# Decoder block: low parts written over the raw weight slabs, six slabs of two buffers, gelu loads one slab ahead

## What is computed

```python
def mixer_sublayer(h, ...):            # h: 16 meta tokens and 512 tokens, D_MODEL = 1024
    z = h @ w_in + b_in                # q, k, v of two attentions, forget gate, two gates
    oa = sliding_window_attention(...)
    ob = forgetting_attention(...)
    merged = sigmoid(ga) * (oa @ w_pa) + sigmoid(gb) * (ob @ w_pb)
    return merged @ w_o

def peer_ffn(h, w_q, sub_keys, u, v):  # 8 heads, 128 x 128 experts, 16 chosen per head
    q = h @ w_q                        # scores of 2 x 128 sub-keys per head
    ...                                # top 16 of each half, top 16 of their sums -> expert, g
    a = gelu(h . u[expert]) * g
    return sum(a * v[expert])
```

## Time and profile before

| | |
|---|---|
| median of 3 runs | 1650.83 us (1649.65 to 1651.99) |
| span of the profiled execution | 1647.4 us |
| PE busy | 1607.1 us, 98% |
| DVE busy | 1333.8 us, 81% |
| ACT busy | 739.8 us, 45% |
| DMA, mean over the span | 266 GB/s |

### The profile page before, as it was taken

How to read it: one execution, slowest core, us unless ns; L and a number is a source line. 1 busy time by engine, 2 the same in 40 slices (tenths; PEclk the granted TensorE clock), 3 DMA queues, 4 the chain that set the end, 5 groups by cost and what they waited for, 6 DMA issues and landing times. The chain is left out here.

```text
span 1647.4 us, 26956 instructions
## 1 busy us (share of the span) xinstructions
PE 1607.1 (98%) x9840; PEld 1487.9 (90%) x9840; DVE 1333.8 (81%) x2850; ACT 739.8 (45%) x1298; POOL 455.8 (28%) x319
## 2 busy tenths in 40 slices
PE   6999999999899999999999999999999999999996
PEld 4897766788788999999999999999999999999996
DVE  4534656565688989999999989769999989898998
ACT  5314644442433535767667744343333333333331
POOL 0000000000011051431233233424554554556740
PEclk9999999999999999999999999999999999999998
DMA  4561111123154596998999899999999999999992
GB/s 150 122 200 39 52 52 52 49 85 98 65 160 135 162 381 209 330 352 255 326 334 341 286 368 340 371 409 378 406 405 405 405 405 403 391 404 400 405 405 102
DMA packets 192500, 438.01 MB, mean 266 GB/s; under 512 B 18744, under 2 KB 102912, under 8 KB 191984
## 3 DMA queue, kind: packets, MB, share of 16 engines
q1 hardware_dynamic: 80928, 226.94, 38.3%
q0 software_dynamic: 44080, 161.06, 26.4%
q10 hardware_dynamic: 67360, 48.28, 8.9%
HBM read 380.08 MB, written 56.13 MB: 265 GB/s over the span
## 5 line engine op out<-in xcount | busy, mean ns | idle before, releaser
L495 PE MATMUL psS<-hT_lo,hi 128*128 128x368 f32 (+2 forms) x1448 | 496.9, 343 | 0.7 <-DVE hT_lo L1111 0.7
L496 PE MATMUL psS<-hT_hi,lo 128*128 128x368 f32 (+2 forms) x1448 | 488.1, 337 | 0.0
L497 PE MATMUL psS<-hT_hi,hi 128*128 128x368 f32 (+2 forms) x1448 | 486.1, 336 | 0.0
L486 DVE TENSOR_TENSOR lo<-raw,hi 128x1024 fp32r<-128x1024 f32 x322 | 393.5, 1222 | 113.2 <-ACT hi L482 105.9
L482 ACT ACTIVATE hi<-raw 128x1024 fp32r<-128x1024 f32 x322 | 339.0, 1053 | 136.5 <-PE psS L497 96.1
L612 POOL DMA_INDIRECT gat<-in_u_rows,idx x144 | 214.7, 1491 | 393.2 <-DVE gat L1290 213.3
L495 PEld LDWEIGHTS psS<-hT_lo,hi 128*128 128x128 f32 x1448 | 272.0, 188 | 23.6 <-issue 11.7
L612 POOL DMA_INDIRECT gat<-in_v_exp,idx x144 | 223.4, 1551 | 228.5 <-DVE gat L1290 146.3
L497 PEld LDWEIGHTS psS<-hT_hi,hi 128*128 128x128 f32 x1448 | 272.2, 188 | 11.6
L496 PEld LDWEIGHTS psS<-hT_hi,lo 128*128 128x128 f32 x1448 | 272.1, 188 | 9.1
L844 ACT ACTIVATE act_hi<-act_t 128x368 fp32r<-128x368 f32 x128 | 65.6, 512 | 289.7 <-DVE act_t L1342 283.1
(11 more groups left out here) (337 smaller groups left out, 2562.1 us busy)
## 6 DMA issues: line engine op xcount, KB each, us to landing
raw<-in_u_exp SPq DMA_DIRECT2D x128, 512.0 KB
raw<-in_v_exp SPq DMA_DIRECT2D x128, 512.0 KB
gelu_dram<-gelu ACTq DMA_DIRECT2D x128, 184.0 KB
gates_dram<-gates ACTq DMA_DIRECT2D x92, 256.0 KB
gel_in<-gelu_dram SPq DMA_DIRECT2D x128, 184.0 KB
raw<-in_w_merge SPq DMA_DIRECT2D x24, 512.0 KB
raw<-in_w_proj SPq DMA_DIRECT2D x18, 512.0 KB
gate_even<-gates_dram SPq DMA_DIRECT2D x24, 384.0 KB
```

What stands on the lines that cost most here:

```text
L486: nc.vector.tensor_tensor(lo[:, n % RING, :], raw[:, n % RING, :], hi[:, n % RING, :].bitcast(F32), ALU.subtract).then_inc(lo_done, 1)
L495: nc.tensor.matmul(out_ap, w_h, x_l, start=start, stop=False)
L496: nc.tensor.matmul(out_ap, w_l, x_h, start=False, stop=False)
L497: return nc.tensor.matmul(out_ap, w_h, x_h, start=False, stop=stop)
```

## The change

`raw` and `lo` are placed at the same address, so that `lo` is written over `raw`, element by element. The memory that three rings of four took now holds two rings of SLABS = 6. A load can no longer go into its buffer when lo(n-4) is done: load n waits until PE has finished slab n-6. hi(n) waits for the landing and for the end of slab n-6 in place of n-4; its place in ACT's program and that of lo(n) in DVE's are as they were. In the v stage the `gel_in` load behind the load of slab v is now that of v+1.

```diff
@@ placing of the buffers
-        raw, hi, lo = place(ctx, raw=([P, RING, D], F32), hi=([P, RING, D], F32R), lo=([P, RING, D], F32R))
+        hi, = place(ctx, hi=([P, SLABS, D], F32R))
+        with ExitStack() as s:
+            raw, = place(s, raw=([P, SLABS, D], F32))
+        lo, = place(ctx, lo=([P, SLABS, D], F32R))
...
         def load(sp, n):
-            if n >= RING:
-                sp.wait_ge(lo_done, n - RING + 1)
-            sp.dma_start(raw[:, n % RING, :], slab_source(n)).then_inc(landed[n % RING], 16)
+            if n >= SLABS:
+                sp.wait_ge(slab_used, n - SLABS + 1)
+            sp.dma_start(raw[:, n % SLABS, :], slab_source(n)).then_inc(landed[n % SLABS], 16)
 
         def split_hi(act, n):
-            act.wait_ge(landed[n % RING], 16 * (n // RING + 1))
-            if n >= RING:
-                act.wait_ge(slab_used, n - RING + 1)
...
+            act.wait_ge(landed[n % SLABS], 16 * (n // SLABS + 1))
+            if n >= SLABS:
+                act.wait_ge(slab_used, n - SLABS + 1)
...
-            for n in range(RING):
+            for n in range(SLABS):
                 load(sp, n)
...
-                if 0 <= v < NKEYS:
-                    sp.wait_ge(gelu_out[v % RING], 16 * (v // RING + 1))
-                    if v >= RING:
-                        sp.wait_ge(act_done, v - RING + 1)
-                    sp.dma_start(gel_in[:, v % RING, :], gelu_dram[v]).then_inc(gel_in_s[v % RING], 16)
+                w = v + 1
+                if 0 <= w < NKEYS:
+                    sp.wait_ge(gelu_out[w % RING], 16 * (w // RING + 1))
+                    if w >= RING:
+                        sp.wait_ge(act_done, w - RING + 1)
+                    sp.dma_start(gel_in[:, w % RING, :], gelu_dram[w]).then_inc(gel_in_s[w % RING], 16)
```

More of the change, by code:

```diff
@@ L41 @@
 RING = 4
+SLABS = 6
 N_PROJ = 18
@@ L406, in build @@
         cst_in, bias_in, x_in, keys_in = sem("cst_in"), sem("bias_in"), [sem(f"x_in{t}") for t in range(5)], sem("keys_in")
-        landed = [sem(f"landed{r}") for r in range(RING)]
+        landed = [sem(f"landed{r}") for r in range(SLABS)]
         hi_done, lo_done, slab_used = sem("hi_done"), sem("lo_done"), sem("slab_used")
@@ L473, in load @@
         def load(sp, n):
-            if n >= RING:
-                sp.wait_ge(lo_done, n - RING + 1)
-            sp.dma_start(raw[:, n % RING, :], slab_source(n)).then_inc(landed[n % RING], 16)
+            if n >= SLABS:
+                sp.wait_ge(slab_used, n - SLABS + 1)
+            sp.dma_start(raw[:, n % SLABS, :], slab_source(n)).then_inc(landed[n % SLABS], 16)
         def split_hi(act, n):
-            act.wait_ge(landed[n % RING], 16 * (n // RING + 1))
-            if n >= RING:
-                act.wait_ge(slab_used, n - RING + 1)
-            nc.scalar.activation(hi[:, n % RING, :], raw[:, n % RING, :], ACT.Copy).then_inc(hi_done, 1)
+            act.wait_ge(landed[n % SLABS], 16 * (n // SLABS + 1))
+            if n >= SLABS:
+                act.wait_ge(slab_used, n - SLABS + 1)
+            nc.scalar.activation(hi[:, n % SLABS, :], raw[:, n % SLABS, :], ACT.Copy).then_inc(hi_done, 1)
         def split_lo(dve, n):
             dve.wait_ge(hi_done, n + 1)
-            nc.vector.tensor_tensor(lo[:, n % RING, :], raw[:, n % RING, :], hi[:, n % RING, :].bitcast(F32),
+            nc.vector.tensor_tensor(lo[:, n % SLABS, :], raw[:, n % SLABS, :], hi[:, n % SLABS, :].bitcast(F32),
                                     ALU.subtract).then_inc(lo_done, 1)
@@ L536, in _ @@
             sp.dma_start(snk[:, 0, :], sinks.partition_broadcast(P)).then_inc(bias_in, 16)
-            for n in range(RING, LAST):
+            for n in range(SLABS, LAST):
                 load(sp, n)
@@ L1496, in _ @@
                 if 1 <= n + 1 <= 4 or 7 <= n + 1 <= 10:
-                    last = slab(n, n % RING, psS[:, n % 2, 0:SEQ], tokens, tokens_lo, all_k)
+                    last = slab(n, n % SLABS, psS[:, n % 2, 0:SEQ], tokens, tokens_lo, all_k)
                 else:
@@ L1501, in _ @@
                         half = slice(b * HALF, (b + 1) * HALF)
-                        last = slab(n, n % RING, psS[:, n % 2, b * SEQ:b * SEQ + HALF], lambda k: hT_hi[:, k, half],
+                        last = slab(n, n % SLABS, psS[:, n % 2, b * SEQ:b * SEQ + HALF], lambda k: hT_hi[:, k, half],
                                     lambda k: hT_lo[:, k, half], all_k)
@@ L1549, in gate_tile @@
                         pe.wait_ge(o_lo_done, 2 * NBLK - 2 + v - SIDE_GATES)
-                last = slab(FIRST_MERGE + v, (FIRST_MERGE + v) % RING, gate_bank(v), tokens, tokens_lo,
+                last = slab(FIRST_MERGE + v, (FIRST_MERGE + v) % SLABS, gate_bank(v), tokens, tokens_lo,
                             [(k, k)], ends=(k == 0, k == KT - 1))
@@ L1622, in _ @@
                     pe.wait_ge(lo_done, n + 1)
-                    slab(n, n % RING, psS[:, 1, SEQ:], tokens, tokens_lo, all_k[:2], ends=(True, False))
+                    slab(n, n % SLABS, psS[:, 1, SEQ:], tokens, tokens_lo, all_k[:2], ends=(True, False))
                 if s >= 2:
@@ L1634, in _ @@
             n = FIRST_MERGE + N_GATE
-            slab(n, n % RING, psS[:, 1, SEQ:], tokens, tokens_lo, all_k[2:], ends=(False, True)).then_inc(slab_used, 1)
+            slab(n, n % SLABS, psS[:, 1, SEQ:], tokens, tokens_lo, all_k[2:], ends=(False, True)).then_inc(slab_used, 1)
             pe.wait_ge(o_lo_done, 2 * NBLK)
@@ L1644, in _ @@
                 for e in range(2):
-                    last = slab(n, n % RING, banks[4 + 2 * (m % 2) + e], lambda k: oT_hi[:, e, k, :],
+                    last = slab(n, n % SLABS, banks[4 + 2 * (m % 2) + e], lambda k: oT_hi[:, e, k, :],
                                 lambda k: oT_lo[:, e, k, :], [(4 * e + k, k) for k in range(4)])
@@ L1666, in _ @@
                         pe.wait_ge(m_lo_done, k + 1)
-                    last = slab(n, n % RING, psS[:, m % 2, 0:SEQ], lambda k: m_hi[:, k, :], lambda k: m_lo[:, k, :],
+                    last = slab(n, n % SLABS, psS[:, m % 2, 0:SEQ], lambda k: m_hi[:, k, :], lambda k: m_lo[:, k, :],
                                 [(k, k)], ends=(k == 0, k == KT - 1))
@@ L1694, in _ @@
                     n = FIRST_PQ + q
-                    last = slab(n, n % RING, pq_bank(q), tokens, tokens_lo, [(k, k)], ends=(k == 0, k == KT - 1))
+                    last = slab(n, n % SLABS, pq_bank(q), tokens, tokens_lo, [(k, k)], ends=(k == 0, k == KT - 1))
                     if k == KT - 1:
@@ L1705, in _ @@
                         pe.wait_ge(pq_lo_done, q - 1 if q >= 6 else q - 3)
-                    slab(n, n % RING, pq_bank(q), tokens, tokens_lo, all_k).then_inc(slab_used, 1)
+                    slab(n, n % SLABS, pq_bank(q), tokens, tokens_lo, all_k).then_inc(slab_used, 1)
                 for c in ((0, 1) if q == 3 else (2, 3) if q == 4 else (q - 1,)):
@@ L1753, in _ @@
                     pe.wait_ge(gelu_done, s - RING + 1)
-                slab(n, n % RING, banks[s % RING][:, 0:DENSE], dense, dense_lo, all_k).then_inc(slab_used, 1)
+                slab(n, n % SLABS, banks[s % RING][:, 0:DENSE], dense, dense_lo, all_k).then_inc(slab_used, 1)
                 if s == FIRST_ROWS:
@@ L1777, in expert_values @@
                         pe.wait_ge(gelu_done, NKEYS - RING + bank + 1)
-                wh, wl = slab_parts(n % RING, m)
+                wh, wl = slab_parts(n % SLABS, m)
                 return split_product(banks[bank][:, 0:DENSE], wh, wl, act_hi[:, v % RING, :], act_lo[:, v % RING, :],
```

## The result

The changed kernel takes 1667.01 us (median of 4 runs, 1665.49 to 1670.15) against 1650.24 us before: a ratio of 1.0109, 95% interval 1.0095 to 1.0122, or about 17 us slower. Its profiled execution has a span of 1663.7 us and a time of 1665.5 us of its own; the span before was 1647.4, so the two traces differ by 16.3 us. Executions in a slow state are left out of every figure; only experiment 11 had any, two of eleven, at 1972.91 and 3838.09 us.

A forecast was written before the change was run, and what follows sets the result against it. PE, busy 98% of the span, was taken as the bound. Terms 0.8 + 2.7 + 1.7 + 0.3 + 3.5 = +9.0 us took the span from 1647.4 to 1656.4, with 3.4 more about 1660 us; range 1646 to 1669.

The forecast's parts named there:

- (a): First stage: slab 13's load, issued later into the w_dram traffic, lands late for PE; +0.8 us, range 0 to 2.
- (b): Decode at turn_keys: now is issued later, so the search of position 16 starts late; +2.7 us, range 0 to +4.0.
- (c): Turn: behind PE's longer wait at 632.10 us the clock drops for twelve matmuls; +1.7 us, range 0 to 1.8.
- (d): Other searches: DVE begins 3.2 us late and lo near 775 us misses PE's need; +0.3 us, range 0 to 1.5.
- (e): v stage: lost prefetch lead and clock, 4.3 + 0.9, less 1.7 for gel order; +3.5 us, range 0 to 6.2.
- The gain of 1.7 for the gel order: v stage: asking for gel_in a slab earlier removes a DVE wait near 1424.98 us; 1.7 us counted as gain.
- The rule on the sharing of the DMA engines: v stage: engines alternate between queue rows with work, so slab loads get about half; lost lead costs 4.3, not 2.1 us.
- A: Rival: the queue absorbs the v stage's lost prefetch, the other terms stay; +5.5 us, 1656.3 us; chance 0.24.
- B: Rival: now lands within 5 us, turn and search costs vanish, nothing visible; 1650 to 1653 us; chance 0.11.
- C: Rival: faster through earlier hi and gel_in, if v loads land in under about 12 us; 1645.8 us; chance 0.16.
- D: Rival: waits on act_lo recur in each group of eight slabs; +16 to +32 us, about 1675; chance 0.07.
- The advice to buffer so that DMA and compute overlap: Skill's double-buffering advice, by which six buffers should hide more than four; weighed against raw slabs held 4.8 us longer.

The follow-up runs named there:

- experiment 11: Kernel with hi in 4 buffers, raw and lo sharing 8, each gel_in load being that of v-1: 1649.19 us, ratio 0.9998 to the kernel before.
- experiment 1: Changed kernel with the memory cut otherwise, hi in 4 buffers and raw and lo sharing 8: 1650.35 us, ratio 1.0007 to the kernel before.
- experiment 6: Changed kernel with 5 shared buffers in place of 6: 1730.62 us, ratio 1.0482 to the kernel before.
- experiment 10: Changed kernel with 4 buffers for hi in place of 6, raw and lo still sharing 6: 1668.22 us, ratio 1.0116 to the kernel before.
- experiment 5: Changed kernel with POOL waiting for hi(16) before it issues the w_dram store: 1678.78 us, ratio 1.0182 to the kernel before.
- experiment 2: Changed kernel with each gel_in load again that of v, not v+1: 1670.09 us, ratio 1.0126 to the kernel before.
- experiment 8: Changed kernel with half of each gathered row of v left out (gathered tokens' output not right): 1655.56 us, ratio 1.0033 to the kernel before.
- experiment 4: Changed kernel with each now load (the scores) issued one slab earlier: 1659.46 us, ratio 1.0072 to the kernel before.
- experiment 9: Kernel before with half of each gathered row of v left out (gathered tokens' output not right): 1641.19 us, ratio 0.9949.
- experiment 3: Kernel before with the gel_in loads one slab ahead (v+1) and nothing else: 1652.21 us, ratio 1.0021.
- experiment 7: Experiment 1 (hi 4 buffers, raw and lo sharing 8) with gel_in again that of v: 1647.25 us, ratio 0.9987 to the kernel before.
- experiment 12: Experiment 7 with 6 gather buffers in place of 7: 1647.19 us, ratio 0.9984 to the kernel before.

## Why the prediction was right, and where its sizes were off

The forecast was slower by 9 us, 1660, in a range of 1646 to 1669; it is slower by 17, 1667.0. The mechanism, loads that go out later because their buffer is freed by PE, holds: experiments 1, 6 and 10 show that the time hangs on when a load may be issued, and on no other part of sharing the memory. Term by term, by the table above:

*(a) First stage, +0.8 taken, 5.0 measured.* This is the step that failed. The prediction took slab 13's load as the first to meet the `w_dram` store. It did not ask the same of slab 12's, which had been issued at 60.15, ahead of the store's start at 64.7, and which moved by 8 us to the other side of it. The range of 0 to 2 was too narrow for the same reason: the price of a moved load is nearly a step, 4 us of duration ahead of the store and 23 behind it, and the earliest load that crosses it sets the bill. The chain behind it (hi, lo, evacuation, PE) was the one predicted, and a clock drop, which the term had left out, came with it. Experiment 5 moves the store and with it the late slab.

*(b, c) Turn, 4.4 taken, 3.5 measured.* `now` at 4.0 us later and a shorter queue were right; the search began 3.5 later against +2.7. PE's wait grew by 2.3 us, and 1.1 us came from a late lo of slab 87 in the same DVE order (PE waited 0.97 us for it at 635.23), which no term had. The clock price of 1.7 was not paid in this execution. It was paid behind a wait of the same length in the traces of experiments 2 (2.5 us), 5, 8 and 10 (1.5 to 1.6 each), so its size was right. That (b) and (c) together still come near the 3.5 is in part luck: the late lo took the place of the clock. Experiment 4 takes all of it back with one digit.

*(d) Other searches, 0.3 taken, 0.9 measured,* 0.4 of it at the place named, lo near 775 us, and 0.4 at the matmuls of the gate matrices 4 us behind it.

*(e) v stage, 3.5 taken, 4.4 measured,* of which the windows show 3.0 from 1212 us on; with the 2.7 to 3.5 of experiments 4, 5 and 10 the forecast is within what single traces scatter. The prediction read the loss before the change a little high: a stretch of 160 us without a wait has 954 matmuls and not 960, so 41 were missing before and not 47, 6.9 us and not 7.8. That DVE and PE lose it to loads in a full queue is shown by experiments 8 and 9, and that it grows with a shorter look-ahead by 6. The gain of 1.7 for the gel order was wrong: the order cost 3 us on the kernel before (3) and on eight shared buffers (1 against 7), and on six neither a gain nor a loss is shown (2). What an earlier `gel_in` saves on itself it puts on hi. The times from issue to use under experiment 7 show why: the earlier `gel_in` waits longer for its own buffer and holds up the slab load behind it on SP, by 1.4 us in experiment 3 and 4.2 in 1, and by nothing with six buffers, where PE's end of a slab comes as late. The term had priced the load that moved, and not the one behind it. The same times give the lost lead: 23.8 us before, 20.5 after, so 3.3 us where the prediction took 5. The rule on the sharing of the DMA engines in the Trainium skill (DMA: Bandwidth & Descriptors, Queues, rings and completion order), by which loads would get half, was weighed in this term. The runs agree with sharing: half the gather bytes halve the time of a slab load, 12.1 to 6.0 us. They don't show the share.

Some 2.4 us more, ahead of the u stage, belong to none of the terms nor to the change (below).

Of the rivals, A (no v loss) and B (nothing visible) are out. C, faster, was to decide if the loads of v land in less than about 12 us. That sign was badly chosen. Of the 90 loads from slab 210 to 299, 14 took longer in the changed kernel (10.2 us on the mean), 46 before (12.1), and 76 in experiment 7 (14.9), which loses least of the three. In a full queue a load that is asked for earlier also stands in it longer, so its duration alone doesn't say whether it is late. Only with half the gathers (experiment 8, no load over 10 us) was nothing lost, and there before the change too (9). D, waits in each group of slabs, is what five buffers do, not six. The advice to buffer so that DMA and compute overlap (the Trainium skill, Trainium Kernel Development and Optimization, Best Practices) says the opposite of the result only if buffers are counted. What overlaps is the time between a load's issue and its use: in the v stage six buffers held until PE's end give 20.5 us of it, four that DVE's lo frees 23.8, and eight 26.9, if no other load on SP holds them up (22.7 where one does).

Open is how much of the 7.2 us that the v stage lost before could be had at all by look-ahead: the best versions here, experiments 7 and 12, are 2 to 3 us better than before, and their intervals end at 1.0000 and 0.9997. Open is also how much of the 17 us between the medians is such a clock event as the last section tells of, since each kernel has only one trace.

## What to carry to other kernels

Count a ring by who frees its buffer and when, not by its buffers, and count what stands ahead of its loads in the same queue with its own wait: write for the old and the new kernel the position at which load n goes out, and do it for all that stands behind it in the same queue. Then take the list of load durations, and ask of each load whether its new time of issue falls into other traffic; the first one that crosses into it takes as long as that traffic does, and what the look-ahead doesn't cover of it is the price (here 23 us in place of 4, of which 5 us with the clock behind it). When memory is freed by sharing, give it to the ring that is held longest (raw and lo here), and none to one whose writer has a fixed place (hi).

## What was not expected of the hardware

The clock behind a wait is not decided by the length of the wait alone. Behind the turn's wait of 3.5 us the granted clock was 1.00 in one kernel and 0.57 in another, with the same program there. Near 427 us, behind a wait of 4.7 us that all kernels have, PE went at half clock for longer in some executions than in others. The windows of 425 to 435 us before and in experiment 1 are these:

```profile
425.00:435.00 10.00, 9.35 (x47) 0.94 0.01 2
```

```profile
425.00:435.00 10.00, 9.35 (x38) 0.76 0.01 2
```

Of the 13 traces beside that of before nine have it, at 1.7 to 2.7 us each, and one of them is experiment 3, where nothing had changed ahead of the place. In the changed kernel it is 2.4. So about 2 of its 16.3 us are such luck, and a single pair of traces of this kernel can't tell differences below that.
